# Differential attention: the second pass of the scores as two products of 64 rows, one on each half of the array

## The chip, the cores and the metric

The kernel runs on one core of a Trainium2 chip. The metric is the device time of the whole program in microseconds, of which less is better. Of the kernel before there are three timed runs, and one more under the hardware profiler, from which all rows below are taken.

## The reference

One layer of an encoder over 2048 tokens of width 1024. Half of the width goes through differential attention, half through dilated windows; then follow an output projection, a squared-ReLU MLP, a gate and a last norm. The change touches the scores of the differential attention alone:

```python
qd = apply_rope(qd.reshape(B, S, N_HEADS_DIFF, 2, HEAD_DIM)...)   # 4 heads, 2 maps each, 64 wide
kd = apply_rope(kd.reshape(B, S, N_HEADS_DIFF, 2, HEAD_DIM)...)
s = jnp.einsum('bhmqd,bhmkd->bhmqk', qblk.astype(jnp.float32) * scale, kf)
pr = jax.nn.softmax(s, axis=-1)
a = pr[:, :, 0] - lam * pr[:, :, 1]
return jnp.einsum('bhqk,bhkd->bhqd', a, vf)
```

For each head and map that is a 2048 x 2048 matrix of dot products over 64 numbers.

## The kernel before, in words

The program is six stages with a barrier between them. The first (`project_phase`) makes q, k and v and stores q and k turned, in DRAM, each as a high part (rounded, in the type that the kernel calls F32R) and a low part (the rest). The second, `differential_phase`, is the one that changes. In the profile its tensors have the prefix `c_`, that of the dilated stage after it `b_`.

The differential stage works through 64 tiles: 4 heads by 16 blocks of 128 queries. A tile has four units, one for each map and each half of the keys (`UNITS`); a unit is the scores of 128 queries against 1024 keys, in two banks of PSUM of 512 columns. There are three such double banks (`RING`), used in turn, for 256 units in all.

A score has 64 products, but the array has 128 rows. Before, the stationary operand `qs` holds q high on rows 0 to 63 and q low on rows 64 to 127; `kt_hi` holds k high on both halves, `kt_lo` k low on both. A product of `qs` with `kt_hi` gives (q high + q low) k high, and one with `kt_lo` adds (q high + q low) k low. So a unit is four products of 128 rows and 512 columns (L739, L740, for the first bank and then the second), each with its own load of the same stationary operand.

TensorE (PE) runs one list in program order. In round n it does for q = 0 to 3: `score(n + 2, q)`, `turn(n, q)` (four transposes of the combined row into one bank, L747) and `values(n - 1, q)` (four products with v, recorded as eight, L758). `score` waits until the exponential of three units ago has been read out of its double bank; `turn(n, 0)` and `turn(n, 2)` wait for a combined half row of VectorE (`S["a"]`).

VectorE (DVE) in round n does `maximum(n + 2, q)` for each unit (L630, waits for the unit's scores), after the first `combine(n, 1)` (L663), after the second and fourth `whole` (L637, the maximum of a map), in the third the result of tile n - 2 and the coefficient of tile n + 1, and last `combine(n + 1, 0)`. ScalarE (ACT) does the four exponentials (L583, each followed by a read of its accumulator), the copies of the transposes to SBUF (`a_copy`, L591) and two small ones. SyncE (SP) issues all DMAs in one list: queries four tiles at a time (`load_q`, two buffers), keys and values a head at a time (`load_k`, `load_v`, two buffers; the first head by `load_k0`, a map at a time), and a store of 64 KB for each tile. Each DMA of q and k fills 32 partitions. PE does not start before the constants have landed (`const_in`), and these are issued behind the first queries and all keys of the first head.

Of the kernel before, what the change touches and what calls it, by code (L numbers as in the profile page):

```python
# [20 lines left out]
P = 128  # L21
SEQ = 2048
# [4 lines left out]
HD = 64  # L27
# [15 lines left out]
F32 = mybir.dt.float32  # L43
F32R = mybir.dt.float32r
# [412 lines left out]
def differential_phase(kit):  # L457


    nc, D = kit.nc, kit.dram  # L460
    HEADS, VD, KT = MAPS // 2, 2 * HD, SEQ // P
    HALF = SEQ // 2
    STEPS = HEADS * TILES
    UNITS = tuple((m, f) for m in range(2) for f in range(2))
    QT = 4 * P
    RING = 3
    with ExitStack() as mem:
        sb = lambda name, shape, dt=F32: mem.enter_context(nc.sbuf_tensor("c_" + name, shape, dt))
# [8 lines left out]
        gain = sb("gain", [P, VD])  # L477
        half = sb("half", [P, 1])
        kt_hi = sb("kt_hi", [P, 2, 2, SEQ], F32R)
        kt_lo = sb("kt_lo", [P, 2, 2, SEQ], F32R)  # L480
        qs = sb("qs", [P, 2, 2, QT], F32R)
        v = sb("v", [P, 2, KT, VD])
        neg_half = sb("neg_half", [P, 2, 2])
        neg_max = sb("neg_max", [P, 2, 2])
# [14 lines left out]
        scores = ps("scores", [P, 2 * RING, 512])  # L499
# [5 lines left out]
        k_in, q_in, stored, v_in = (kit.sem_pair("c_" + s) for s in ("k_in", "q_in", "stored", "v_in"))  # L505
        k0_in = kit.sem_pair("c_k0_in")
# [7 lines left out]
        with nc.Block() as block:  # L514

            @block.sync
            def _(sp):
                def rows(g, h, ab, u):
                    return D["qkt"][0, g, h // 2, ab, u, h % 2 * HD:h % 2 * HD + HD].rearrange("(m d) s -> d m s", d=32)

                def load_q(m):
                    if m >= 2:
                        sp.wait_ge(S["scored"], 4 * 4 * (m - 1))
                    for k in range(4):
                        sp.dma_start(qs[32 * k:32 * k + 32, m % 2].bitcast(F32),
                                     rows(0, m // 4, k % 2, k // 2)[:, :, m % 4 * QT:m % 4 * QT + QT]
                                     ).then_inc(q_in[m % 2], 16)

                def load_k(h):
                    if h >= 2:  # L530
                        sp.wait_ge(S["scored"], 4 * TILES * (h - 1))
                    for u, kt in enumerate((kt_hi, kt_lo)):
                        for k in range(4):
                            sp.dma_start(kt[32 * k:32 * k + 32, h % 2].bitcast(F32),
                                         rows(1, h, k % 2, u)).then_inc(k_in[h % 2], 16)

                def load_k0(m):
                    for u, kt in enumerate((kt_hi, kt_lo)):
                        for k in range(4):
                            sp.dma_start(kt[32 * k:32 * k + 32, 0, m].bitcast(F32),  # L540
                                         rows(1, 0, k % 2, u)[:, m]).then_inc(k0_in[m], 16)

                def load_v(h):
                    if h >= 2:
                        sp.wait_ge(S["pv"], 4 * TILES * (h - 1))
                    sp.dma_start(v[:, h % 2], D["vd"][:, h * VD:(h + 1) * VD].rearrange("(t p) d -> p t d", p=P)
                                 ).then_inc(v_in[h % 2], 16)

                def store(n):
                    h, t = n // TILES, n % TILES  # L550
                    sp.wait_ge(S["out"], n + 1)
                    sp.dma_start(D["od"][t * P:(t + 1) * P, h * VD:(h + 1) * VD], out[:, n % 2]).then_inc(stored[n % 2], 16)

                load_q(0)
                load_k0(0)
                load_k0(1)
                sp.dma_start(ident[:], D["ident"][:]).then_inc(const_in, 16)
                for k, name in enumerate(("lambda_q1", "lambda_k1", "lambda_q2", "lambda_k2")):
                    sp.dma_start(lam_in[:, k], D[name][0].partition_broadcast(P)).then_inc(const_in, 16)
                sp.dma_start(gain_in[:], D["g_subln"].partition_broadcast(P)).then_inc(const_in, 16)  # L560
                load_q(1)
                load_v(0)
                load_k(1)
                load_v(1)
                for n in range(STEPS + 3):
                    if n % 4 == 2 and n // 4 + 2 < STEPS // 4:
                        load_q(n // 4 + 2)
                    if n >= 3:
                        store(n - 3)
                    if n % TILES == 4 and n >= TILES and n // TILES + 1 < HEADS:  # L570
                        load_k(n // TILES + 1)
                        load_v(n // TILES + 1)
                for s in range(2):
                    sp.wait_ge(stored[s], 16 * STEPS // 2)
# [147 lines left out]
            @block.tensor  # L722
            def _(pe):
                def score(n, u):
                    m, f = UNITS[u]
                    h, t, U = n // TILES, n % TILES, 4 * n + u
                    if u == 0:
                        pe.wait_ge(q_in[n // 4 % 2], 64 * (n // 8 + 1))
                    if n == 0 and f == 0:
                        pe.wait_ge(k0_in[m], 128)  # L730
                    if h and t == 0 and u == 0:
                        pe.wait_ge(k_in[h % 2], 128 * ((h + 1) // 2))
                    if U >= RING:
                        pe.wait_ge(S["exp"], U - RING + 1)
                    queries = qs[:, n // 4 % 2, m, t % 4 * P:t % 4 * P + P]
                    for b in range(2):
                        cols = slice(f * HALF + b * 512, f * HALF + b * 512 + 512)
                        found = scores[:, U % RING * 2 + b]
                        nc.tensor.matmul(found, queries, kt_hi[:, h % 2, m, cols], start=True, stop=False)  # L739
                        ins = nc.tensor.matmul(found, queries, kt_lo[:, h % 2, m, cols], start=False, stop=True)  # L740
                    ins.then_inc(S["scored"], 1)

                def turn(n, g):
                    pe.wait_ge(S["a"], 2 * n + g // 2 + 1)
                    pe.wait_ge(S["at"], 4 * n + g)
                    for c in range(4):
                        ins = nc.tensor.transpose(turned[:, c * P:(c + 1) * P],  # L747
                                                  a_row[:, n % 2, (4 * g + c) * P:(4 * g + c + 1) * P], ident[:])
                    ins.then_inc(S["a_turned"], 1)

                def values(n, g):
                    h, s = n // TILES, n % 2
                    if g == 0:
                        pe.wait_ge(S["o"], n)
                        pe.wait_ge(v_in[h % 2], 16 * (h // 2 + 1))
                    pe.wait_ge(S["at"], 4 * n + g + 1)
                    for c in range(4 * g, 4 * g + 4):
                        ins = nc.tensor.matmul(pv[:, :VD], at[:, s, c], v[:, h % 2, c], start=(c == 0), stop=(c == KT - 1))  # L758
                    ins.then_inc(S["pv"], 1)

                pe.wait_ge(const_in, 96)
                for n in range(-2, STEPS + 1):
                    for q in range(4):
                        if n + 2 < STEPS:
                            score(n + 2, q)
                        if 0 <= n < STEPS:
                            turn(n, q)
                        if 0 <= n - 1 < STEPS:
                            values(n - 1, q)
# [1137 lines left out]


PHASES = (project_phase, differential_phase, dilated_phase, mix_phase, mlp_phase, gate_phase)


# [63 lines left out]
```

## Time and profile before

| what | us |
|---|---|
| three timed runs, median | 3663.91 |
| lowest and highest of them | 3659.92 and 3665.02 |
| the profiled execution's own time | 3657.93 |
| its span, first to last instruction | 3656.1 |
| its mean granted TensorE clock | 0.972 of full |

The span is what the rows below divide up. PE is the row of the array's products, PEld that of its weight loads, and both can run at once. The end of a product in the records is modelled: it is shown until its last result has left the array, while the next one may have started long before, so the distance from start to start says what a product costs in a stream. A granted clock of 1.00 is 2.4 GHz, 0.50 is 1.2 GHz. Times in a timeline are microseconds from the start of the span. The differential stage has its first score product at 601 and its last at 1218.

### The profile page before, as it was taken

Reading aid. Unit: us, or ns where it says so; the run is one execution under the profiler, and the core shown is the slowest. Engines: PE = TensorE matmul, PEld = TensorE weight load, DVE = VectorE, ACT = ScalarE, POOL = GpSimd, SP = SyncE. Lnnn points to the kernel's source line nnn. Section 1 sums busy time; section 2 is a strip of 40 time slices with the busy share of each in tenths; the row PEclk is TensorE's granted clock in tenths of the full one; section 3 lists DMA queues with packets and bytes.
Section 4 is the critical chain, followed back from the end, with each engine's and each line's share of the span. In section 5 each row is a group of like instructions: output and inputs, shape, how many; then the busy total and the mean of one; then the engine's idle time right before and its main releaser. Section 6 shows DMA issues by size and latency. Waiting matters only on the chain. (4 is left out here: it accounts for less than half of the span.)

```text
span 3656.1 us, 51666 instructions
## 1 busy us (share of the span) xinstructions
PE 3391.8 (93%) x18272; PEld 2919.9 (80%) x18272; DVE 1795.1 (49%) x3370; ACT 1317.4 (36%) x2718; POOL 630.6 (17%) x694
## 2 busy tenths in 40 slices
PE   8999995999999699993997999999999999997798
PEld 8988883888888699993776888888888888885677
DVE  5124344888888588883443333333343333333333
ACT  4111112777777577771222122121222112211332
POOL 2023330111111100001221222222222222221122
PEclk9999997999999899996998999999999999998899
DMA  5233336012300466744556111111231111112332
GB/s 184 98 107 125 118 107 167 19 46 56 77 19 19 104 145 163 174 116 141 184 173 208 57 46 46 46 46 52 83 124 46 47 56 46 46 46 113 104 108 90
DMA packets 279064, 342.75 MB, mean 94 GB/s; under 512 B 75248, under 2 KB 209264, under 8 KB 273648
## 3 DMA queue, kind: packets, MB, share of 16 engines
q1 hardware_dynamic: 278896, 340.59, 31.2%
q8 instruction: 96, 1.57, 0.2%
q14 instruction: 72, 0.59, 0.1%
HBM read 243.66 MB, written 96.86 MB: 93 GB/s over the span
## 5 line engine op out<-in xcount | busy, mean ns | idle before, releaser
L1553 DVE TENSOR_TENSOR e_h<-e_down_acc,e_h 128x512 f32<-128x512 f32 x512 | 350.4, 690 | 847.4 <-PE e_down_acc L89 847.4
L87 PE MATMUL e_up_acc<-e_xt_hi,e_up_hi 128*128 128x512 f32 x1024 | 399.3, 390 | 20.4 <-DVE e_xt_lo L1530 20.4
L88 PE MATMUL e_up_acc<-e_xt_lo,e_up_hi 128*128 128x512 f32 x1024 | 399.1, 390 | 0.0
L89 PE MATMUL e_up_acc<-e_xt_hi,e_up_lo 128*128 128x512 f32 x1024 | 399.0, 390 | 0.0
L87 PE MATMUL e_down_acc<-e_down_hi,e_u_hi 128*128 128x512 f32 x1024 | 398.3, 389 | 0.0
L88 PE MATMUL e_down_acc<-e_down_lo,e_u_hi 128*128 128x512 f32 x1024 | 398.3, 389 | 0.0
L89 PE MATMUL e_down_acc<-e_down_hi,e_u_lo 128*128 128x512 f32 x1024 | 398.3, 389 | 0.0
L630 DVE TENSOR_REDUCE c_neg_half<-c_scores 128x1 f32<-128x1024 f32 x256 | 313.1, 1223 | 84.7 <-PE c_scores L740 84.7
L1573 POOL TENSOR_TENSOR e_sq<-e_r 128x512 f32<-128x512 f32 x128 | 133.7, 1045 | 1006.8 <-ACT e_r L1509 1006.8
L583 ACT ACTIVATE c_e<-c_scores,c_neg_max 128x1024 f32<-128x1024 f32 x256 | 287.1, 1122 | 19.4 <-DVE c_neg_max L637 11.5
L758 PE MATMUL c_pv<-c_v,c_at 128*128 128x128 f32 x2048 | 270.1, 275 | 0.4 <-ACT c_o L597 0.4
L739 PE MATMUL c_scores<-c_kt_hi,c_qs 128*128 128x512 f32 x512 | 225.1, 440 | 40.8 <-DMA c_gain_in<-g_subln_dram 35.1
L1503 ACT CAST e_down_hi<-e_down_raw 128x2048 fp32r<-128x2048 f32 x32 | 61.2, 1913 | 537.8 <-PE e_down_acc L89 536.2
L758 PEld LDWEIGHTS c_pv<-c_v,c_at 128*128 128x128 f32 x2048 | 248.6, 192 | 0.5 <-ACT c_o L597 0.5
L87 PEld LDWEIGHTS e_up_acc<-e_xt_hi,e_up_hi 128*128 128x128 f32 x1024 | 192.7, 188 | 61.1 <-issue 20.7
L1018 PE MATMUL b_scores<-b_kt,b_qs 128*128 128x256 f32 x768 | 207.0, 402 | 23.0 <-DMA b_masks<-masks_dram 23.0
L89 PEld LDWEIGHTS e_up_acc<-e_xt_hi,e_up_lo 128*128 128x128 f32 x1024 | 192.6, 188 | 40.1
L88 PEld LDWEIGHTS e_up_acc<-e_xt_lo,e_up_hi 128*128 128x128 f32 x1024 | 192.6, 188 | 40.0
L89 PEld LDWEIGHTS e_down_acc<-e_down_hi,e_u_lo 128*128 128x128 f32 x1024 | 192.2, 188 | 39.9
L88 PEld LDWEIGHTS e_down_acc<-e_down_lo,e_u_hi 128*128 128x128 f32 x1024 | 192.2, 188 | 39.9
L87 PEld LDWEIGHTS e_down_acc<-e_down_hi,e_u_hi 128*128 128x128 f32 x1024 | 192.2, 188 | 39.9
L1509 ACT ACTIVATE e_r<-e_up_acc 128x512 f32<-128x512 f32 x128 | 76.7, 599 | 393.8 <-PE e_up_acc L89 393.8
(162 smaller groups left out, 7149.7 us busy)
## 6 DMA issues: line engine op xcount, KB each, us to landing
s_qkt<-a_hl SPq DMA_DIRECT2D x128, 256.0 KB, 2.8
e_up_raw<-w_up_dram SPq DMA_DIRECT2D x32, 1024.0 KB, 5.8
e_down_raw<-w_down_dram SPq DMA_DIRECT2D x32, 1024.0 KB, 4.9
b_kt<-s_qkt SPq DMA_DIRECT2D x64, 256.0 KB, 10.8
a_w_raw<-w_in_dram SPq DMA_DIRECT2D x24, 512.0 KB, 5.4
d_nd<-s_nd SPq DMA_DIRECT2D x48, 256.0 KB, 4.1
s_vg<-a_hl SPq DMA_DIRECT2D x32, 256.0 KB, 2.0
c_qs<-s_qkt SPq DMA_DIRECT2D x64, 128.0 KB, 2.8
```

The lines of the kernel that those rows point to most:

```text
L87: nc.tensor.matmul(out, lhs_hi, rhs_hi, start=first, stop=False)
L88: nc.tensor.matmul(out, lhs_hi, rhs_lo, start=False, stop=False)
L89: return nc.tensor.matmul(out, lhs_lo, rhs_hi, start=False, stop=last)
L583: nc.scalar.activation(e[:, n % 2, m, f * HALF:(f + 1) * HALF], bank(n, u), ACT.Exp, bias=neg_max[:, n % 2, m:m + 1], accum_out=sums[:, n ...
L630: nc.vector.tensor_reduce(neg_half[:, m, f:f + 1], bank(n, u), AX.X, ALU.max, negate=True).then_inc(S["halved"], 1)
L739: nc.tensor.matmul(found, queries, kt_hi[:, h % 2, m, cols], start=True, stop=False)
L758: ins = nc.tensor.matmul(pv[:, :VD], at[:, s, c], v[:, h % 2, c], start=(c == 0), stop=(c == KT - 1))
L1018: ins = nc.tensor.matmul(dst, queries, keys, start=(u == 0), stop=(u == 1))
L1503: nc.scalar.copy(down_hi[:], down_raw[:]).then_inc(S["down_hi"], 1)
L1509: nc.scalar.activation(r[:, k % 2], up_acc[:, k % 2], ACT.Relu).then_inc(S["relu"], 1)
L1553: nc.vector.tensor_tensor(h[:, slot(z, t), cols], down_acc[:, k % 4], h[:, slot(z, t), cols], ALU.add).then_inc(S["h"], 1)
L1573: nc.gpsimd.tensor_tensor(sq[:, k % 2], r[:, k % 2], r[:, k % 2], ALU.mult).then_inc(S["sq"], 1)
```

## The change

The second pass no longer uses `qs`. A new tensor `q_hi` holds q high on rows 0 to 63 and again on rows 64 to 127. `kt_lo` shrinks to half its columns: of each 1024 keys, rows 0 to 63 hold k low of the first 512 and rows 64 to 127 k low of the second 512. A unit is now two products of 128 rows (`qs` with `kt_hi`, one for each bank, L744) and then two of 64 rows, the first on the upper half of the array into the first bank, the second on the lower half into the second bank (L748). The term q low times k low, which was part of the sum before, is no longer computed. For the 64-row products the program's instructions carry a tile of 64 x 128 at rows 0 and 64 of the array; every other product of the program keeps the whole array.

The loads follow: `load_q` issues eight DMAs instead of four, and `load_map` issues for each group of 32 partitions one DMA of k high and one of k low, k low as two runs of 512 columns for each row. The keys after the first head come a map at a time, in 16 DMAs instead of 8 larger ones.

```diff
         kt_hi = sb("kt_hi", [P, 2, 2, SEQ], F32R)
-        kt_lo = sb("kt_lo", [P, 2, 2, SEQ], F32R)
+        kt_lo = sb("kt_lo", [P, 2, 2, HALF], F32R)
         qs = sb("qs", [P, 2, 2, QT], F32R)
+        q_hi = sb("q_hi", [P, 2, 2, QT], F32R)
...
                     for k in range(4):
-                        sp.dma_start(qs[32 * k:32 * k + 32, m % 2].bitcast(F32),
-                                     rows(0, m // 4, k % 2, k // 2)[:, :, m % 4 * QT:m % 4 * QT + QT]
-                                     ).then_inc(q_in[m % 2], 16)
+                        for t, u in ((qs, k // 2), (q_hi, 0)):
+                            sp.dma_start(t[32 * k:32 * k + 32, m % 2].bitcast(F32),
+                                         rows(0, m // 4, k % 2, u)[:, :, m % 4 * QT:m % 4 * QT + QT]
+                                         ).then_inc(q_in[m % 2], 16)
+
+                def load_map(h, m, done):
+                    for k in range(4):
+                        sp.dma_start(kt_hi[32 * k:32 * k + 32, h % 2, m].bitcast(F32),
+                                     rows(1, h, k % 2, 0)[:, m]).then_inc(done, 16)
+                        low = rows(1, h, k % 2, 1)[:, m].rearrange("d (f b c) -> d f b c", f=2, b=2)
+                        sp.dma_start(kt_lo[32 * k:32 * k + 32, h % 2, m].rearrange("d (f c) -> d f c", f=2).bitcast(F32),
+                                     low[:, :, k // 2]).then_inc(done, 16)
...
-                    for u, kt in enumerate((kt_hi, kt_lo)):
-                        for k in range(4):
-                            sp.dma_start(kt[32 * k:32 * k + 32, h % 2].bitcast(F32),
-                                         rows(1, h, k % 2, u)).then_inc(k_in[h % 2], 16)
+                    for m in range(2):
+                        load_map(h, m, k_in[h % 2])
...
                 def load_k0(m):
...
+                    load_map(0, m, k0_in[m])
...
-                    queries = qs[:, n // 4 % 2, m, t % 4 * P:t % 4 * P + P]
+                    tokens = slice(t % 4 * P, t % 4 * P + P)
+                    found = [scores[:, U % RING * 2 + b] for b in range(2)]
                     for b in range(2):
                         cols = slice(f * HALF + b * 512, f * HALF + b * 512 + 512)
-                        found = scores[:, U % RING * 2 + b]
-                        nc.tensor.matmul(found, queries, kt_hi[:, h % 2, m, cols], start=True, stop=False)
-                        ins = nc.tensor.matmul(found, queries, kt_lo[:, h % 2, m, cols], start=False, stop=True)
+                        nc.tensor.matmul(found[b], qs[:, n // 4 % 2, m, tokens], kt_hi[:, h % 2, m, cols],
+                                         start=True, stop=False)
+                    for b in range(2):
+                        side = slice(b * HD, (b + 1) * HD)
+                        ins = nc.tensor.matmul(found[b], q_hi[side, n // 4 % 2, m, tokens],
+                                               kt_lo[side, h % 2, m, f * 512:(f + 1) * 512], start=False, stop=True)
                     ins.then_inc(S["scored"], 1)
```

On PE, a unit of a tile in the middle of the stage, with the transposes and value products behind it and the next unit's scores, reads before (c_turned is the bank of the transposes, c_pv that of the value products):

```order
L739 MATMUL c_scores<-c_kt_hi,c_qs 128x512
L740 MATMUL c_scores<-c_kt_lo,c_qs 128x512
L739 MATMUL c_scores<-c_kt_hi,c_qs 128x512
L740 MATMUL c_scores<-c_kt_lo,c_qs 128x512
L747 MATMUL c_turned<-c_ident,c_a_row 128x128 x4
L758 MATMUL c_pv<-c_v,c_at 128x128 x4
L739 MATMUL c_scores<-c_kt_hi,c_qs 128x512
```

The same place on PE now:

```order
L744 MATMUL c_scores<-c_kt_hi,c_qs 128x512 x2
L748 MATMUL c_scores<-c_kt_lo,c_q_hi 128x512 x2
L756 MATMUL c_turned<-c_ident,c_a_row 128x128 x4
L767 MATMUL c_pv<-c_v,c_at 128x128 x4
L744 MATMUL c_scores<-c_kt_hi,c_qs 128x512 x2
```

There are still four products of 512 columns in a unit; the two with k high now stand first, the two of 64 rows (shown by their output, 128x512) behind them, directly ahead of the transposes. The lists of DVE, ACT and POOL keep their order.

On SP, the start of the stage reads before (the row of the constants follows it):

```order
L525 DMA c_qs<-s_qkt 32x2x512 x4
L540 DMA c_kt_hi<-s_qkt 32x2048 x4
L540 DMA c_kt_lo<-s_qkt 32x2048 x4
L540 DMA c_kt_hi<-s_qkt 32x2048 x4
L540 DMA c_kt_lo<-s_qkt 32x2048 x4
L557 DMA c_ident<-ident_dram 128x128
```

The same place on SP now, its first twelve DMAs:

```order
L527 DMA c_qs<-s_qkt 32x2x512
L527 DMA c_q_hi<-s_qkt 32x2x512
L527 DMA c_qs<-s_qkt 32x2x512
L527 DMA c_q_hi<-s_qkt 32x2x512
L527 DMA c_qs<-s_qkt 32x2x512
L527 DMA c_q_hi<-s_qkt 32x2x512
L527 DMA c_qs<-s_qkt 32x2x512
L527 DMA c_q_hi<-s_qkt 32x2x512
L533 DMA c_kt_hi<-s_qkt 32x2048
L536 DMA c_kt_lo<-s_qkt 32x2x512
L533 DMA c_kt_hi<-s_qkt 32x2048
L536 DMA c_kt_lo<-s_qkt 32x2x512
```

The pair of k high and k low stands eight times, and then come the constants: 24 DMAs ahead of them instead of 20.

## Rows read from the trace of the kernel before

**Rows 1.** The page, part 1: busy us (share of the span) and instructions.

```profile
PE 3391.8 (93%) x18272; PEld 2919.9 (80%) x18272; DVE 1795.1 (49%) x3370; ACT 1317.4 (36%) x2718; POOL 630.6 (17%) x694
```

**Rows 2.** The windows: stretch, its length, busy us and count by engine, PEclk, DMA share, GB/s.

```profile
640.00:1218.00 578.00, 550.71 (x3812) 480.21 (x3811) 493.13 (x716) 443.14 (x894) 64.00 (x180) 1.00 0.15 38
615.00:620.00 5.00, 2.62 (x10) 1.61 (x11) 4.07 (x8) 3.06 (x6) 0.26 (x1) 1.00 1.04 221
585.00:590.00 5.00, 0.00 (x0) 0.00 (x0) 0.00 (x0) 0.00 (x0) 0.00 (x0) 0.50 1.02 223
```

**Rows 3.** The waits in 640 to 1218: us in total, times, longest us.

```profile
ACT c_at L591 <- PE c_turned L747: 106.6, 178, 0.7
DVE c_neg_half L630 <- PE c_scores L740: 76.5, 179, 0.8
PE c_turned L747 <- DVE c_a_row L663: 27.3, 59, 0.5
```

**Rows 4.** The timeline of PE: start, us, engine, line, operation, tiles, count, idle before.

```profile
1201.65 0.66 PE L747 MATMUL c_turned<-c_ident,c_a_row 128*128 128x128 f32 x4 [0.46 <-DVE c_a_row L663]
...
1202.95 0.47 PE L739 MATMUL c_scores<-c_kt_hi,c_qs 128*128 128x512 f32 x1
1203.27 0.39 PE L740 MATMUL c_scores<-c_kt_lo,c_qs 128*128 128x512 f32 x1
1203.50 0.40 PE L739 MATMUL c_scores<-c_kt_hi,c_qs 128*128 128x512 f32 x1
1203.73 0.39 PE L740 MATMUL c_scores<-c_kt_lo,c_qs 128*128 128x512 f32 x1
1203.96 0.60 PE L747 MATMUL c_turned<-c_ident,c_a_row 128*128 128x128 f32 x4
...
1207.47 0.48 PE L739 MATMUL c_scores<-c_kt_hi,c_qs 128*128 128x512 f32 x1
...
1208.25 0.40 PE L740 MATMUL c_scores<-c_kt_lo,c_qs 128*128 128x512 f32 x1
...
1211.36 0.65 PE L747 MATMUL c_turned<-c_ident,c_a_row 128*128 128x128 f32 x4 [0.46 <-DVE c_a_row L663]
```

**Rows 5.** The timeline of the weight loads beside one unit of these.

```profile
1202.92 0.19 PEld L739 LDWEIGHTS c_scores<-c_kt_hi,c_qs 128*128 128x128 f32 x1
1203.04 0.19 PEld L740 LDWEIGHTS c_scores<-c_kt_lo,c_qs 128*128 128x128 f32 x1
1203.27 0.19 PEld L739 LDWEIGHTS c_scores<-c_kt_hi,c_qs 128*128 128x128 f32 x1
1203.50 0.19 PEld L740 LDWEIGHTS c_scores<-c_kt_lo,c_qs 128*128 128x128 f32 x1
```

**Rows 6.** The timeline of DVE in the same tile.

```profile
1204.16 1.23 DVE L630 TENSOR_REDUCE c_neg_half<-c_scores 128x1 f32<-128x1024 f32 x1 [0.24 <-PE c_scores L740]
...
1206.42 1.22 DVE L630 TENSOR_REDUCE c_neg_half<-c_scores 128x1 f32<-128x1024 f32 x1 [0.84 <-PE c_scores L740]
...
1208.68 1.23 DVE L630 TENSOR_REDUCE c_neg_half<-c_scores 128x1 f32<-128x1024 f32 x1 [0.20 <-PE c_scores L740]
...
1210.02 1.28 DVE L663 SCALAR_TENSOR_TENSOR c_a_row<-c_e,c_coef 128x1024 f32<-128x1024 f32 x1
```

**Rows 7.** The timeline of ACT in the same tile: one exponential and its accumulator.

```profile
1205.62 1.12 ACT L583 ACTIVATE c_e<-c_scores,c_neg_max 128x1024 f32<-128x1024 f32 x1
1206.63 0.19 ACT L583 ACTIVATION_READ_ACCUMULATOR c_e<-c_scores,c_neg_max 128x1 f32 x1
```

**Rows 8.** The timeline of SP's queue at the stage's start.

```profile
575.17 1.73 SPq L525 DMA_DIRECT2D c_qs<-s_qkt  x4
...
586.74 0.43 SPq L560 DMA_DIRECT2D c_gain_in<-g_subln_dram  x1
```

**Rows 9.** The timeline of PE there: the first product of the stage.

```profile
600.95 0.80 PE L739 MATMUL c_scores<-c_kt_hi,c_qs 128*128 128x512 f32 x1 [35.08 <-DMA c_gain_in<-g_subln_dram]
```

**Rows 10.** The DMA issues in 560 to 640: count, KB each, us to landing.

```profile
c_kt_hi<-s_qkt SPq DMA_DIRECT2D x8, 256.0 KB, 8.2
c_kt_lo<-s_qkt SPq DMA_DIRECT2D x8, 256.0 KB, 11.1
c_qs<-s_qkt SPq DMA_DIRECT2D x12, 128.0 KB, 2.9
```

More of the change, by code:

```diff
@@ L531, in load_k @@
                         sp.wait_ge(S["scored"], 4 * TILES * (h - 1))
-                    for u, kt in enumerate((kt_hi, kt_lo)):
-                        for k in range(4):
-                            sp.dma_start(kt[32 * k:32 * k + 32, h % 2].bitcast(F32),
-                                         rows(1, h, k % 2, u)).then_inc(k_in[h % 2], 16)
+                    for m in range(2):
+                        load_map(h, m, k_in[h % 2])
                 def load_k0(m):
[L538 to L541, printed above, removed]
+                    load_map(0, m, k0_in[m])
                 def load_v(h):
@@ L727, in score @@
                     if u == 0:
-                        pe.wait_ge(q_in[n // 4 % 2], 64 * (n // 8 + 1))
+                        pe.wait_ge(q_in[n // 4 % 2], 128 * (n // 8 + 1))
                     if n == 0 and f == 0:
@@ L731, in score @@
                     if h and t == 0 and u == 0:
-                        pe.wait_ge(k_in[h % 2], 128 * ((h + 1) // 2))
+                        pe.wait_ge(k_in[h % 2], 256 * ((h + 1) // 2))
                     if U >= RING:
                         pe.wait_ge(S["exp"], U - RING + 1)
-                    queries = qs[:, n // 4 % 2, m, t % 4 * P:t % 4 * P + P]
+                    tokens = slice(t % 4 * P, t % 4 * P + P)
+                    found = [scores[:, U % RING * 2 + b] for b in range(2)]
                     for b in range(2):
                         cols = slice(f * HALF + b * 512, f * HALF + b * 512 + 512)
-                        found = scores[:, U % RING * 2 + b]
-                        nc.tensor.matmul(found, queries, kt_hi[:, h % 2, m, cols], start=True, stop=False)
-                        ins = nc.tensor.matmul(found, queries, kt_lo[:, h % 2, m, cols], start=False, stop=True)
+                        nc.tensor.matmul(found[b], qs[:, n // 4 % 2, m, tokens], kt_hi[:, h % 2, m, cols],
[4 more added lines that the diff above has]
+                                               kt_lo[side, h % 2, m, f * 512:(f + 1) * 512], start=False, stop=True)
                     ins.then_inc(S["scored"], 1)
```

## The prediction

> **What bounds the kernel now.** I read the page first. TensorE is busy in 93% of the span [rows 1], so products are the program's currency; but the change touches one stage, and its limit has to be read there. The windows come next: from 640 to 1218 the stage is in a steady state, at full clock (1.00, 2.4 GHz), with the DMA engines at 0.15 and PE busy in 551 of 578 us, DVE in 493, ACT in 443 [rows 2]. The waits say how it is closed: PE waits 59 times, in all 27.3 us, always for DVE's combined half row, and DVE waits 179 times (three in a tile), in all 76.5 us, always for scores [rows 3]. Two engines that wait for each other once a tile are one loop, and the loop can be walked in the timelines.
>
> Start at the transposes of a tile's first quarter, at 1201.65. The next scores begin 1.30 later, at 1202.95. Two whole units (scores, transposes, values) take 4.52, to 1207.47. The fourth product of the third unit starts 0.78 after that, at 1208.25 [rows 4]. DVE takes the maximum 0.43 later, at 1208.68, and begins the combination 1.34 after that, at 1210.02 [rows 6]; the next tile's transposes start 1.34 later, at 1211.36 [rows 4]. Sum: 1.30 + 4.52 + 0.78 + 0.43 + 1.34 + 1.34 = 9.71 us a tile. 578 / 9.71 is 59.5, which fits the 59 waits; I count 60 tiles. So the loop contains the scores of three units. The fourth unit's scores run while DVE works on the combination, and what is saved there becomes a longer wait of PE. A unit cheaper by d makes a tile cheaper by 3d, and the stage by 180d.
>
> **The scores.** Nothing is taken out in number: four products and four weight loads a unit, before and after. What changes is that the last two may run beside each other. Before, products of 512 columns start 0.23 apart (1203.27, 1203.50, 1203.73), and the transposes 0.23 behind the last; the first product is followed after 0.32, because its weight load (1202.92) came late and the next started only 0.12 behind it [rows 4, 5]. So third and fourth product cost 0.46 together. If they stream fully side by side they cost 0.23, d = 0.23.
>
> Can both start at once? Each needs its own load first. In rows 5 every load starts exactly at the start of the product ahead of it (1203.27, 1203.50: the same times as in rows 4), never two ahead. With that habit the third product's load is hidden under the second product, but the fourth's starts with the third product, and is through 0.12 later, which is the distance of the first two loads. The fourth product then starts 0.12 behind the third instead of 0.23, and the transposes 0.23 behind the fourth: the pair costs 0.35, d = 0.11 to 0.12. No row shows a product of 64 rows, so the bounds are wide: from above d = 0.23 (full overlap); from below, that the two run one after the other (d = 0) and that the change of the array's form costs something each way, up to d = -0.33 (worked out under the rivals). I take 0.12, because it follows from how loads behave in this very loop. 60 x 3 x 0.12 = 21.6 us.
>
> The array can run two such products at once by the Trainium skill too (TensorEngine Tiling, Key Properties): different tiles load weights and multiply in parallel. No row here shows it.
>
> **What is late next.** The wait of DVE is 76.5 / 59.5 = 1.29 a tile [rows 3], so DVE's own work is about 8.4 of 9.71, and a tile of 9.35 leaves it room on average. In place: counted from the transposes, the second unit's scores come 0.12 earlier (DVE had waited 0.24), the third's 0.24 earlier (of 0.84), the fourth's 0.36. There DVE had waited 0.20 and is itself 0.24 earlier, so it could start 0.44 earlier: 0.36 goes through [rows 6]. With d = 0.23 the fourth comes 0.69 earlier, DVE is ready 0.23 to 0.24 (limited by the third, which gives 0.46) + 0.20 earlier: 0.66 at most. So full overlap gives 0.66 a tile, not 0.69. ACT: the exponential whose bank the last scores of the tile need runs from 1205.62 and is read by 1206.82, 0.65 before these scores start at 1207.47 [rows 4, 7]; it moves earlier by d, the scores by 2d, so 0.65 - d is left. ACT waits 106.6 / 59.5 = 1.8 a tile for transposes [rows 3], and is no bound either.
>
> **The loads.** At the start PE waits for the constants until 600.95 [rows 9], and these lie behind all loads of the first head: before 4 x 128 KB of q and 16 x 256 KB of k [rows 10], 4.5 MB; now 1 MB of q, 2 MB of k high and 1 MB of k low, 4 MB. At 223 GB/s [rows 2] half a megabyte is 2.3 us. Against it: four more DMAs at 0.43 us [rows 8] move the constants' issue by 1.7 us, to some 588.5, still long before they would land; and k low comes in 2 KB runs rather than 8 KB ones. How much slower these go no row tells; between nothing and the whole gain back, and 2 us more, the term is -2.3 to +2. I take -1. In the steady state the next head's 4 MB of keys become 3 MB, the queries double to 1 MB in 39 us, at a DMA share of 0.15: hidden. SP's list is one queue: 16 key DMAs take 16 x 0.47 = 7.5 us instead of 3.8, and what stands behind them is a tile's store, due one tile (9.7 us) later, whose buffer DVE wants two tiles later. If the queue fills up it may take twice that, and still nothing waits. Bound: 0 to 5 us for the heads after the second.
>
> Before 640 the pipeline fills; there the exponentials pace it, and I count nothing. The clock stays at 1.00 with PE busy for 2.62 of 5 us [rows 2], far less than the loop will have, so shorter streaming does not cost clock.
>
> **The sum.** -21.6 - 1 = -23 us, against this execution's own 3657.93: 3635. That execution is 6 us under the median of the timed runs, 3663.91; against the median it is 3641, which I forecast.
>
> **The rivals.** (A) Both loads are brought in ahead and the pair streams fully side by side: 60 x 0.66 = 40 us and the 1 of the start, 3623. For it: the second load goes to rows of the array that the third product doesn't use. Against: rows 5. The Trainium skill says just this (TensorE: Matmul & The Clock Gate, The mechanism, of packed tiles): loads to other row groups are pulled ahead, and products then start some 4 ns apart. By that rule it is this rival; the trace, with whole-array loads only, neither bears it out nor speaks against it.
>
> (B) The array must be emptied when its form changes, at the second product's end and again ahead of the transposes. A product's last result is out 0.39 to 0.40 after its start, and the next starts after 0.23 [rows 4]: emptying costs 0.16 to 0.17 each time. Twice that is 0.33, less the 0.23 of full overlap: d = -0.10, 180 x 0.10 = +18 us, less 1: 3681. It decides from 0.115 a switch on, where the sum is zero. (C) is the harder form, in which the weight load too waits for the empty array: twice 0.11 to 0.12 more, d = -0.33, +59 us, 3722. For both: two switches in each of 256 units. Against: none of the program's products has this form, so no row can show it. The Trainium skill states that rule (TensorEngine Tiling, Key Properties): "Changing tiling mode (not just tile) drains the TensorE". It gives no price; by the rows' 0.16 it would turn the gain into a loss.
>
> (D) The halves take turns after all, or a mild emptying eats just the overlap: d = 0 within 0.03, 3663 within 5.
>
> **How the numbers follow.** Forecast 0.35 (with mild emptying in it, 3632 to 3653), A 0.22, B 0.20, C 0.12, D 0.11. Some 0.2%, 7 us, is what a measurement tells from no change. Faster by more: the forecast and A, 0.57, and 0.01 of D. Same: 0.10 of D, 0.02 each of the forecast's edge and B. Slower: B and C, less the edge, 0.30. That makes 0.56, 0.14, 0.30. The range goes from below A to within reach of C, leaving out most of C and a little below A: 3614 to 3700; the forecast's own is 3632 to 3653.
>
> **What would show it.** In the timeline of a unit after: starts of L744 0.32 apart, the first L748 0.23 behind, the second L748 0.12 behind that (A: some hundredths; D: 0.23), the transposes 0.23 behind the second. Under B the gap from the second L744 to the first L748 is about 0.4, under C about 0.5, and again ahead of the transposes. A tile takes 9.35 (A 9.05, B 10.0, C 10.7); DVE's wait for scores falls by 3 x 0.12 a tile, to some 55 us, and PE's wait for DVE rises by 0.12 a tile. The first product of the stage starts within 599 to 603. The prediction is wrong if the loop's starts show another distance, or if DVE waits for a store's buffer.

## The result and the profile after

The change made the kernel slower: 3675.66 us median of six runs (3673.28 to 3677.79) against 3662.91 us for six runs of the kernel before (3655.97 to 3665.02), a ratio of 1.0038 with a 95% interval of 1.0025 to 1.0051. The forecast was 3641. The profiled execution took 3676.62 us with a span of 3674.8 at a mean granted clock of 0.970. That is 18.7 us more than the profiled execution of the kernel before, which lay 5 us under its median; the medians are 12.75 apart.

I read the steady state of the differential stage first, as before. This is its window after, and the waits in it (columns as in [rows 2, 3]):

```profile
640.00:1218.00 578.00, 558.01 (x3728) 411.90 (x3727) 482.96 (x698) 431.56 (x872) 62.09 (x174) 1.00 0.19 47
```

```profile
ACT c_at L596 <- PE c_turned L756: 128.6, 233, 0.7
DVE c_neg_half L635 <- PE c_scores L748: 87.0, 174, 1.0
PEld c_scores L748 <- issue: 84.8, 233, 0.4
...
PEld c_turned L756 <- issue: 28.7, 116, 0.2
PE c_turned L756 <- DVE c_a_row L668: 20.3, 59, 0.3
```

The same 578 us hold fewer instructions on every engine (PE 3728 against 3812 [rows 2]), and DVE waits longer for scores, 87.0 against 76.5 [rows 3], where 55 was forecast. The third and fourth rows are new: weight loads that start late though nothing in the profile holds them, 233 times for the 64-row pair, 0.36 us each. Something between two products holds up the loads, and with them the products. The timeline of PE shows where, over one turn of the loop that answers to [rows 4]:

```profile
1196.08 0.66 PE L756 MATMUL c_turned<-c_ident,c_a_row 128*128 128x128 f32 x4 [0.34 <-DVE c_a_row L668]
...
1197.39 0.71 PE L744 MATMUL c_scores<-c_kt_hi,c_qs 128*128 128x512 f32 x2
1198.03 0.50 PE L748 MATMUL c_scores<-c_kt_lo,c_q_hi 64*128 64x512 f32 x2
1198.46 0.66 PE L756 MATMUL c_turned<-c_ident,c_a_row 128*128 128x128 f32 x4
...
1202.15 0.71 PE L744 MATMUL c_scores<-c_kt_hi,c_qs 128*128 128x512 f32 x2
1202.79 0.50 PE L748 MATMUL c_scores<-c_kt_lo,c_q_hi 64*128 64x512 f32 x2
1203.22 0.66 PE L756 MATMUL c_turned<-c_ident,c_a_row 128*128 128x128 f32 x4
1203.71 1.06 PE L767 MATMUL c_pv<-c_v,c_at 128*128 128x128 f32 x8
...
1206.01 0.66 PE L756 MATMUL c_turned<-c_ident,c_a_row 128*128 128x128 f32 x4 [0.34 <-DVE c_a_row L668]
```

Two products that stand in one row (x2) and last 0.50 in all, where one alone lasts about 0.5 here, start together: the records of the two have starts 0.004 us apart. So the halves overlap fully. But the pair starts 0.64 after the first full product (0.31 to the second, then 0.33), and the transposes start 0.43 behind the pair. The loads of the same unit, against [rows 5]:

```profile
1202.12 0.30 PEld L744 LDWEIGHTS c_scores<-c_kt_hi,c_qs 128*128 128x128 f32 x2
1202.79 0.19 PEld L748 LDWEIGHTS c_scores<-c_kt_lo,c_q_hi 64*128 64x128 f32 x2 [0.36 <-issue]
1203.22 0.42 PEld L756 LDWEIGHTS c_turned<-c_ident,c_a_row 128*128 128x128 f32 x4 [0.25 <-issue]
```

Before, each load started with the product ahead of it and was hidden. Now the loads of the pair start with the pair (1202.79), and that of the transposes with the transposes (1203.22). And the maxima and the combination on DVE, for the end of the loop in [rows 6]:

```profile
1203.33 1.23 DVE L635 TENSOR_REDUCE c_neg_half<-c_scores 128x1 f32<-128x1024 f32 x1 [0.31 <-PE c_scores L748]
...
1204.67 1.29 DVE L668 SCALAR_TENSOR_TENSOR c_a_row<-c_e,c_coef 128x1024 f32<-128x1024 f32 x1
```

The walk of the prediction, with the numbers of after: from the transposes at 1196.08 to the scores 1.31, two units 4.76 (2.38 each, to 1202.15), to DVE's maximum 1.18, to the combination 1.34, to the transposes 1.34: 9.93 us a tile against 9.71. A unit became 0.12 longer. The scores of the unit that ends the loop are ready 0.03 sooner, 1.18 against 0.78 + 0.43 = 1.21. So 2 x 0.12 - 0.03 and a rounding remainder of 0.01 make 0.22.

The 0.12 of a unit can be read from the same rows. The pair starts 0.33 behind the second full product, where the next product had started after 0.23: +0.10. The transposes start 0.43 behind the pair, where full overlap alone would give 0.23: +0.20. The value products start 0.49 behind the transposes (1203.22 to 1203.71). Before it was 0.44, from 1203.96 [rows 4] to this row:

```profile
1204.40 1.06 PE L758 MATMUL c_pv<-c_v,c_at 128*128 128x128 f32 x8
```

That is +0.05, and 0.35 in all for going into the 64-row form and out again; the overlap gives back 0.23, and 0.12 is left.

Where the 18.7 us of the two profiled executions went: from DVE's first score maximum to its last 615.2 before and 631.3 after, +16.1, of which 60 x 0.22 = 13.2 lie in the steady state and 2.9 in its fill; the first score product came 1.2 earlier. That is 14.9. The rest, 3.8, lies in the later stages, which have no edit; from the dilated stage's first product to the last product of the program the unchanged code took 2385.5 before, 2389.3 after, and 2378.0 to 2390.5 in the other kernels here. No run tells more about it.

### The profile page after: what moved, and what is told of

The parts are those of the page before. It is cut to its first block and busy times, and to the rows that moved or that the text cites. A ratio compares the mean times of both kernels' runs of the same rounds, so it can differ in the third digit from the quotient of the medians.

```text
span 3674.8 us, 51754 instructions
## 1 busy us (share of the span) xinstructions
PE 3418.9 (93%) x18272; PEld 2858.5 (78%) x18272; DVE 1794.8 (49%) x3370; ACT 1315.6 (36%) x2718; POOL 630.7 (17%) x694
## 5 line engine op out<-in xcount | busy, mean ns | idle before, releaser
L744 PE MATMUL c_scores<-c_kt_hi,c_qs 128*128 128x512 f32 x512 | 187.6, 448 | 36.7 <-DMA c_gain_in<-g_subln_dram 33.8
```

Of the source, the lines that this page charges most:

```text
L744: nc.tensor.matmul(found[b], qs[:, n // 4 % 2, m, tokens], kt_hi[:, h % 2, m, cols], start=True, stop=False)
```

## The experiments

Theory S (switch): the halves overlap fully, but every change between products of 128 and of 64 rows lets the array run empty and shows a weight load; the loop passes through two units whole and through one without its second change. Its rivals: the new order of the products, the 64-row loads, the new DMAs, or a loss spread over all units alike. Kernels with a ratio were timed against the kernel before on the same chip, where its median lay between 3655.49 and 3660.61. x_bench, x_u0, x_u1 and x_u3 ran once each, under the profiler; of these I use the trace and not the time. The units of a tile are numbered 0 to 3. The loop holds units 1, 2 and 3 and ends with the scores of unit 3; unit 0 is the one outside.

**x_bench: the price by itself.** The kernel before, with a stage behind it in which PE alone runs patterns (`full` is 128 rows; `upper`, `lower` are 64 rows on either half; `above` is the upper half again, into other banks):

```diff
+                for _ in range(16):
+                    full(0); full(1); upper(0); lower(1)
+                for _ in range(16):
+                    full(0); full(1); above(2); above(3)
+                for _ in range(24):
+                    upper(0); lower(1)
...
+                for _ in range(16):
+                    full(0); full(1); turns()
+                for _ in range(16):
+                    upper(0); lower(1); turns()
+                for _ in range(12):
+                    full(0); full(1); full(0); full(1); upper(0); lower(1); upper(0); lower(1)
```

> The kernel before, with a seventh stage behind it that computes nothing for the output: PE alone runs eight patterns of products of 512 columns without waits. Theory S (switch): the two 64-row products overlap fully, but each change of the array's form lets the array run empty and shows a weight load. Then full, full, upper, lower takes about 1.07 us a group (upper and lower 0.00 apart; 0.33 from the second full to upper, 0.43 from lower to the next full, 0.31 between the fulls); upper, lower alone, with no change of form, takes 0.23 a pair, half of two fulls (0.46); two 64-row products in the same half take 0.46 a pair. Full, full, four transposes takes 0.90 a group; upper, lower, four transposes about 0.9 to 1.0 in spite of the overlap, since it changes form twice. Rival O (order): nothing is lost in a change of form, and what the stage lost comes from its waits: full, full, upper, lower takes 0.69 a group. Rival L (loads): the loads of 64 rows are slow in themselves; then upper, lower alone takes clearly over 0.23 a pair as well.

The timeline of PE in the first, second, third and last of these patterns (L1934 full, L1937 upper, L1940 lower, L1943 above):

```profile
3682.05 0.73 PE L1934 MATMUL t_acc<-t_x,t_w 128*128 128x512 f32 x2
3682.72 0.49 PE L1937 MATMUL t_acc<-t_x,t_w 64*128 64x512 f32 x1
3682.72 0.49 PE L1940 MATMUL t_acc<-t_x,t_w 64*128 64x512 f32 x1
3683.14 0.73 PE L1934 MATMUL t_acc<-t_x,t_w 128*128 128x512 f32 x2
...
3699.92 0.73 PE L1934 MATMUL t_acc<-t_x,t_w 128*128 128x512 f32 x2
3700.58 0.73 PE L1943 MATMUL t_acc<-t_x,t_w 64*128 64x512 f32 x2
3701.24 0.73 PE L1934 MATMUL t_acc<-t_x,t_w 128*128 128x512 f32 x2
...
3720.64 0.39 PE L1937 MATMUL t_acc<-t_x,t_w 64*128 64x512 f32 x1
3720.69 0.39 PE L1940 MATMUL t_acc<-t_x,t_w 64*128 64x512 f32 x1
3720.87 0.39 PE L1937 MATMUL t_acc<-t_x,t_w 64*128 64x512 f32 x1
3720.91 0.39 PE L1940 MATMUL t_acc<-t_x,t_w 64*128 64x512 f32 x1
...
3770.76 1.19 PE L1934 MATMUL t_acc<-t_x,t_w 128*128 128x512 f32 x4
...
3772.54 1.20 PE L1934 MATMUL t_acc<-t_x,t_w 128*128 128x512 f32 x4
```

And the two with four transposes behind the products (L1947 `turns`), first after two full products, then after a pair:

```profile
3735.36 0.60 PE L1947 MATMUL t_flip<-t_ident,t_row 128*128 128x128 f32 x4
...
3736.26 0.60 PE L1947 MATMUL t_flip<-t_ident,t_row 128*128 128x128 f32 x4
...
3750.82 0.66 PE L1947 MATMUL t_flip<-t_ident,t_row 128*128 128x128 f32 x4
...
3751.83 0.66 PE L1947 MATMUL t_flip<-t_ident,t_row 128*128 128x128 f32 x4
```

By the starts: full, full, upper, lower takes 1.09 a group (3682.05 to 3683.14), against 4 x 0.227 = 0.91 for four fulls (48 of them alone, ahead of these patterns, follow each other by 0.227 at full clock). Upper and lower alone take 0.23 a pair (3720.64 to 3720.87): the overlap is worth its full 0.23 and the 64-row loads cost nothing, which ends rival L.

Full, full, above, above changes form as often and overlaps nothing: 1.32 a group (3699.92 to 3701.24). Over all groups of a pattern the means are 1.323 and 0.907, so between full products two changes cost 0.416, 0.21 each, and the overlap gives back 0.23. In the patterns without a full product the half of the array changes from product to product and nothing is lost, so the price is that of the form and not of the half.

The 0.21 can be split by the stage's own records: the pair's loads start 0.33 behind the second full product, where the product itself could have started at 0.23. That is 0.10 in which nothing starts, and I read it as the array running empty. Then a load of 0.11 ([rows 5]: two loads follow each other by 0.12) lies open. The rows show the 0.33; that the first part of it is emptying is argued.

Over four fulls and two pairs the two changes are shared: 1.78 (3770.76 to 3772.54) for the work of eight products, against 1.82 in fulls. So two pairs to a visit of the other form about break even.

With four transposes behind, as in the stage, a group took 0.90 after two fulls (3735.36 to 3736.26) and 1.01 after a pair (3750.82 to 3751.83): a loss of 0.11, or 0.34 for the two changes less 0.23. That is the 0.12 and the 0.35 of the stage. It is less than 0.42 because a part of the second change's open load doesn't show in the time from the transposes to what follows (0.05 instead of 0.11 in the stage).

**x_order: the order alone.** Four full products, k high twice and then k low twice:

```diff
...
-                        nc.tensor.matmul(found, queries, kt_hi[:, h % 2, m, cols], start=True, stop=False)
-                        ins = nc.tensor.matmul(found, queries, kt_lo[:, h % 2, m, cols], start=False, stop=True)
+                    for kt, first in ((kt_hi, True), (kt_lo, False)):
+                        for b in range(2):
...
+                            ins = nc.tensor.matmul(scores[:, U % RING * 2 + b], queries, kt[:, h % 2, m, cols],
+                                                   start=first, stop=not first)
```

> The kernel before with the order of the kernel after alone: all four products of 128 rows, the two with k high first, then the two with k low. Theory S: the order costs nothing, a tile stays at 9.71 us, ratio to before 1.000 within 0.002. Rival O: a part of the 0.22 us a tile shows here, a tile takes 9.8 to 9.93, ratio up to 1.004.

A tile took 9.71 us and the ratio was 1.000 (0.999 to 1.0009). The order costs nothing.

**x_half: the changes of form without the overlap.**

```diff
+                    upper = q_hi[0:HD, n // 4 % 2, m, t % 4 * P:t % 4 * P + P]
...
+                        nc.tensor.matmul(scores[:, U % RING * 2 + b], queries, kt_hi[:, h % 2, m, parts[b]],
+                                         start=True, stop=False)
+                    for b in range(2):
+                        ins = nc.tensor.matmul(scores[:, U % RING * 2 + b], upper, kt_lo[0:HD, h % 2, m, parts[b]],
+                                               start=False, stop=True)
```

> The kernel after with both 64-row products on the upper half of the array (k low for all keys on rows 0 to 63, loaded as before), so that they cannot overlap but change the array's form as often. Theory S: the pair costs 0.23 more than after, a unit 2.61 instead of 2.38, a tile 9.93 + 3 x 0.23 = 10.62, some 54 us slower than before, ratio 1.015. If there was no overlap in the kernel after either, a tile stays at 9.93 and the ratio at 1.004.

A tile took 10.61 us, as expected; the ratio was 1.0185 (1.0168 to 1.0202), more than the 1.015 expected. 60 x 0.90 is 54 of the 68 us; the first four tiles took another 10, with the clock at 1.2 GHz still longer (below), and the start was 1.8 later. So the overlap is real in the stage too, and worth 0.68 us a tile.

**x_lowfirst: the pair ahead of the full products.**

```diff
+                        side = slice(b * HD, (b + 1) * HD)
+                        nc.tensor.matmul(found[b], q_hi[side, n // 4 % 2, m, tokens],
+                                         kt_lo[side, h % 2, m, f * 512:(f + 1) * 512], start=True, stop=False)
...
-                        nc.tensor.matmul(found[b], qs[:, n // 4 % 2, m, tokens], kt_hi[:, h % 2, m, cols],
-                                         start=True, stop=False)
...
-                        ins = nc.tensor.matmul(found[b], q_hi[side, n // 4 % 2, m, tokens],
-                                               kt_lo[side, h % 2, m, f * 512:(f + 1) * 512], start=False, stop=True)
+                        ins = nc.tensor.matmul(found[b], qs[:, n // 4 % 2, m, tokens], kt_hi[:, h % 2, m, cols],
+                                               start=False, stop=True)
```

> The kernel after with the 64-row pair ahead of the two full products in each unit. Theory S: still two changes of form a unit, one now between the value products and the pair, one between the pair and the full products; the transposes start 0.23 behind the last full product with their load hidden, but the scores end later, by 0.15 to 0.2, since both changes now lie ahead of their end. A tile takes 10.0 to 10.3, ratio 1.005 to 1.011. Rival O (no price of a change, only its place beside the transposes hurts): a tile takes 9.7 or less.

A tile took 10.21 us, ratio 1.0093 (1.0077 to 1.011). Both changes now lie ahead of the end of the scores, and DVE gets them later. So the loss is not one of the place beside the transposes alone, where 9.7 or less was the rival's number.

**x_u0, x_u1, x_u3: one unit of four.** The pair in one unit of each tile alone (k loaded as before, q high as after):

```diff
+                        side = slice(b * HD, (b + 1) * HD) if u in (1,) else slice(0, P)
+                        low = (q_hi if u in (1,) else qs)[side, n // 4 % 2, m, tokens]
+                        ins = nc.tensor.matmul(scores[:, U % RING * 2 + b], low, kt_lo[side, h % 2, m, parts[b]],
+                                               start=False, stop=True)
```

> The kernel before with the 64-row pair in the first unit of each tile alone. Theory S with the loop: this unit's scores run while VectorE works on the combination that PE then waits for, so its 0.12 us is covered: a tile stays at 9.71. Together with the second and fourth units alone (9.83 and 9.68) and a third unit like the second: 0 + 0.12 + 0.12 - 0.03 = 0.21, the 0.22 of the kernel after. Rival (a quarter each): 9.77.

> The kernel before with the 64-row pair in the second unit of each tile alone (map 0, second half of the keys); the other units use four products of 128 rows. Theory S with the loop: this unit lies inside the loop with all of its 0.12 us, so a tile takes 9.71 + 0.12 = 9.83 us. Rival (the loss comes from the whole stage, a quarter from each unit): 9.71 + 0.22 / 4 = 9.77.

> The same with the pair in the fourth unit alone. Theory S with the loop: the loop leaves TensorE at the end of these scores, which come 0.03 us earlier (overlap less the first change of form); the second change lies behind that end and is covered by the wait for the combined row. A tile takes 9.68 to 9.70 us. Rival (a quarter from each unit): 9.77.

The tiles took 9.71 (x_u0), 9.83 (x_u1) and 9.68 us (x_u3). x_u0 loads q high as the kernel after does and loses nothing a tile, so these loads don't cost in the loop. The row of the wait that ends the loop, in x_u1 and then in x_u3:

```profile
1005.79 0.66 PE L754 MATMUL c_turned<-c_ident,c_a_row 128*128 128x128 f32 x4 [0.46 <-DVE c_a_row L665]
...
1015.62 0.66 PE L754 MATMUL c_turned<-c_ident,c_a_row 128*128 128x128 f32 x4 [0.46 <-DVE c_a_row L665]
```

```profile
1001.41 0.66 PE L754 MATMUL c_turned<-c_ident,c_a_row 128*128 128x128 f32 x4 [0.32 <-DVE c_a_row L665]
...
1011.09 0.66 PE L754 MATMUL c_turned<-c_ident,c_a_row 128*128 128x128 f32 x4 [0.31 <-DVE c_a_row L665]
```

From row to row 9.83 and 9.68; in x_u3 the wait shrank from 0.46 to 0.32, because the second change of form took its place. The same edit is worth 0, +0.12 or -0.03 us a tile by where it stands in the loop, and the rival of equal shares (9.77 each) falls. With unit 2 like unit 1, which was not tried alone, they add up to 0.21 of the 0.22.

**x_u0123: the new loads of k taken away.** The same edit for all four units.

> The pair in all four units, with k loaded as in the kernel before (both halves whole, 8 large DMAs a head) and q high as in the kernel after. It separates the new loads from the products. Theory S: a tile takes 9.93 as in the kernel after, the clock stays at 1.2 GHz until about 625 as there, ratio to before 1.004 to 1.006, the start 1 to 4 us later than in the kernel after because 0.5 MB more than before lie ahead of the constants. Rival (the loads carry a part): 9.8 or less a tile.

A tile took 9.93 us, the ratio was 1.0052 (1.0035 to 1.0069), and the first score product came at 604.0 (602.7 in x_half, which loads the same) instead of 599.7. So the 0.22 a tile is the products' alone, and the smaller k low is worth 3 to 4 us of the start against loading q high beside a whole k low (603 to 604 against 599.7).

**The clock in the fill.** The windows from 605 to 620 of before, after, x_order, x_early_before, x_u0123 and x_early_after (the last two kernels are below; PEclk is the third number from the end):

```profile
605.00:620.00 15.00, 8.91 (x29) 5.23 (x28) 10.77 (x16) 8.11 (x14) 0.26 (x1) 0.89 1.03 217
```

```profile
605.00:620.00 15.00, 11.88 (x26) 4.71 (x24) 9.23 (x14) 7.74 (x13) 0.26 (x1) 0.50 1.05 225
```

```profile
605.00:620.00 15.00, 9.61 (x31) 5.43 (x31) 11.31 (x16) 8.10 (x14) 0.26 (x1) 0.84 1.03 217
```

```profile
605.00:620.00 15.00, 10.54 (x33) 6.30 (x33) 11.81 (x17) 8.37 (x15) 0.26 (x1) 0.84 1.03 216
```

```profile
605.00:620.00 15.00, 12.36 (x28) 5.05 (x27) 8.70 (x10) 5.90 (x11) 0.00 (x0) 0.50 1.08 240
```

```profile
605.00:620.00 15.00, 12.35 (x28) 5.21 (x26) 10.13 (x14) 6.90 (x12) 0.26 (x1) 0.50 1.07 247
```

The stage starts at 1.2 GHz after the wait for its loads. With full products alone it rises some 5 us into the stage (before, 0.50 in 599 to 604 and 0.84 in 604 to 609); in all six kernels with 64-row products in every unit (after, x_half, x_lowfirst, x_u0123, x_dve_after, x_early_after) it stands at 0.50 throughout this window, though PE is shown busy for longer. In none of the others does it; with the pair in one unit of four (x_u0, x_u1, x_u3) it is 0.67 to 0.78. That goes with the 2.9 us of the fill. No run takes the clock apart from the rest of the fill, so the size is an attribution.

**x_dve_before, x_dve_after: the loop opened.** If the loss depends on a loop with DVE, another order on DVE must change it. Here the combination stands ahead of the fourth maximum:

```diff
+                        if q == 3 and 0 <= n + 1 < STEPS:
+                            combine(n + 1, 0)
                         if n + 2 < STEPS:
                             maximum(n + 2, q)
...
-                        if q == 3 and 0 <= n + 1 < STEPS:
-                            combine(n + 1, 0)
```

> The kernel before with VectorE's order changed in one place: the first combination of the next tile stands ahead of the fourth maximum instead of behind it. Theory S with the loop: this opens the loop, PE no longer waits for the combined row, and a tile takes PE's own 4 x 2.26 = 9.03 us: 40 us faster than before, ratio 0.989. Rival: the fourth maximum now comes later, the exponentials behind it too, and the loop closes elsewhere: 9.3 us or more.

> The kernel after with the same change of VectorE's order. Theory S: all four units now count with both changes of form, so a tile takes 4 x 2.38 = 9.52 us, 0.48 more than x_dve_before instead of the 0.22 between before and after; ratio to before about 0.997. Rival (the 64-row pair costs 0.22 a tile whatever the loop): 0.22 more than x_dve_before, about 9.25, ratio 0.993.

The first of these missed: 9.50 us a tile and 0.9957 (0.994 to 0.9973), since the delayed maximum closed the loop again through the exponentials, as its rival said (PE waited 58 times for an exponential). x_dve_after took 9.59 and 0.9981 (0.9972 to 0.9991), with no wait of PE for an exponential or a combined row in the list, but 0.07 above the 9.52 that PE alone would give. The difference of 0.09 was neither the 0.48 of theory S nor the 0.22 of its rival: the first of the two was bound by the exponentials and not by PE, so the pair decided nothing.

**x_early_before, x_early_after: opened for good.** The small operations that make the coefficient go ahead of the third maximum, into a wait of 0.84 us [rows 6], and the combination directly behind that maximum:

```diff
+                        if q == 2 and 0 <= n + 1 < STEPS:
+                            denominators(n + 1)
+                            reciprocal(n + 1)
+                            coefficient(n + 1)
                         if n + 2 < STEPS:
                             maximum(n + 2, q)
...
                         if q == 2 and n >= 2:
                             result(n - 2)
                         if q == 2 and 0 <= n + 1 < STEPS:
-                            denominators(n + 1)
-                            reciprocal(n + 1)
-                            coefficient(n + 1)
-                        if q == 3 and 0 <= n + 1 < STEPS:
                             combine(n + 1, 0)
```

> The kernel before with VectorE's small operations for the next tile's coefficient ahead of the third maximum (where it had waited 0.84 us) and the first combination behind the third maximum. Theory: the loop is open at last, no wait closes it again, PE bound: 9.03 to 9.1 us a tile, 37 to 40 us faster than before, ratio 0.989 to 0.990. Rival: the delay of the fourth maximum (about 0.4 us) again makes the exponentials late: 9.3 or more, ratio 0.993 or more.

> The kernel after with the same order of VectorE. Theory S: PE bound, 4 x 2.38 = 9.52 us a tile, 0.48 more than x_early_before, 29 us or more slower than it. Rival (0.22 whatever the loop): 9.25.

Both came out as theory S had them: 9.04 and 9.52 us a tile, the second 0.48 more and not 0.22. The window of x_early_before, from 640 to 1180:

```profile
640.00:1180.00 540.00, 539.37 (x3819) 485.50 (x3817) 489.24 (x716) 441.17 (x894) 63.97 (x180) 1.00 0.16 41
```

PE is busy in 539.37 of 540 us. x_early_before took 3612.55 us median, ratio 0.9885 (0.9869 to 0.9902) to the kernel before: it beats both kernels of this case. With the 64-row pair the same order took 3641.92, ratio 0.9963 (0.9949 to 0.9977), 29 us more. Once PE is the bound, all four units pay 0.12, 0.48 us a tile, twice the 0.22 that the change cost in the kernel as it stood.

## Why the prediction was wrong

**What bounds the stage** was right: the loop of 9.71 us, the three units in it and the one outside were confirmed by x_u0 (outside, 9.71), x_u1 (inside, 9.83), x_u3 (at the end, 9.68) and by x_early_before and x_early_after. Unit 2 was not tried alone.

**The scores** failed: a unit was to become 0.12 us cheaper and became 0.12 dearer (2.38 against 2.26). Two steps were wrong. The first was that "every load starts exactly at the start of the product ahead of it", from which the fourth product was to trail by 0.12: its start trailed by 0.004, and the pair overlapped for its full 0.23. The rows had only whole-array loads, and the habit does not hold across the halves; rival A had this right. The Trainium skill says that such packed products start some 4 ns apart (TensorE: Matmul & The Clock Gate, The mechanism); the trace agrees with 0.004 us. The second step was the heavier: I put the change of the array's form at nothing in the forecast (in the chances stands "mild emptying in it", in the sum nothing) and left it to the rivals; the third product's load was to be hidden under the second product and wasn't. In the stage the two changes cost 0.35 us a unit against the 0.23 of the overlap, and between full products in x_bench 0.21 each. The Trainium skill says that the array drains when the tiling mode changes (TensorEngine Tiling, Key Properties); the traces agree so far as each change costs time, 0.21 us in x_bench. PE's wait for DVE, which was to rise by 0.12 a tile, fell instead, from 27.3 to 20.3 us.

**Rival B** came nearest. It priced a change at 0.16 to 0.17, from the end of the last result; two of them were 0.33, and the stage's rows show 0.35, for another reason: 0.10 in which nothing starts, and a load that lies open, which only rival C had. C priced the load at its full 0.11 to 0.12 on top of B's emptying, 0.56 for both changes, and was too dear. B gave a tile of 10.0 and 3681 us where 9.93 and 3675.66 were measured. That it was so near is partly luck: the price fitted though its make-up did not, and the rule of 3d, which made B too dear, is wrong for a cost that stands behind the scores; the 2.9 us of the fill and the 3.8 of the later stages were in no sum. In the unit that ends the loop only the first change counts, and that is outweighed by the overlap (-0.03). The loop's rule should have been applied to each instruction, not to the unit.

**What is late next** did not arise with the slower unit, and was not tested for a faster one.

**The loads**: -1.2 us measured for the start against -1, and no wait of DVE for a store's buffer stands in the waits after.

**The fill** was counted at nothing, and took 2.9 more. "Shorter streaming does not cost clock" held for the steady state (1.00); in the fill the clock was at 0.50 until past 620, with full products at 0.84 to 0.89 on average from 605 on. That this is where the 2.9 come from is not shown.

**The chances**: slower had 0.30 and faster 0.56. What weighed wrongly was a lack of rows. I took the absence of any 64-row product in the trace as a ground against the drain, although it was as much a ground against a cheap change. Rivals B and C deserved a larger share than 0.32.

## What to carry to other kernels

Two half-array products do run at once, but a visit to the half-array form cost 0.42 us in and out between full products (x_bench) and 0.35 ahead of the transposes (kernel after), at full clock, where an overlapped pair of 512 columns gives back 0.23. One pair a visit lost in both places, and two pairs between full products about broke even (1.78 against 1.82); more than two were not tried. Group such products, or keep the program in one form. And before pricing an edit, place it in the loop that sets the period: the same edit gave 0, +0.12 and -0.03 us a tile in three places. Here three small instructions and a combination, moved on VectorE into a wait and ahead of a maximum, were worth 43 us (3612.55 against 3655.49), over three times what the change lost.

## What the runs showed of the hardware that was not expected

- In the first score units, started at 1.2 GHz, the granted clock did not rise for more than 15 us with 64-row pairs in every unit, with PE shown busy in 11.88 of 15 us (605 to 620 in the kernel after); with full products it was at 0.84 to 0.89 on average in the same window, with 8.91 to 10.54 busy.
- The 64-row pair's two loads are recorded 0.003 us apart, where two loads of the whole array follow each other by 0.11 to 0.12.
- Behind a change of form the first product is recorded at the start of its load: in x_bench the next full one follows after 0.34 instead of 0.23, the 0.11 of a load more. So a timeline there seems to show a product 0.11 before it runs. It is the same behind a wait: the transposes at 1201.65 in the kernel before are recorded with their load, which starts at 1201.64.
